# The last chunk of a two-layer block: its attention spread out, its sums, memory part and query products placed later

## What is computed

```python
h = rmsnorm(x, norm_mix_g[l])
p_conv, p_attn, p_ssm = jnp.split(h @ w_in[l], ...)
y_conv = conformer_conv(p_conv, ...)        # sigmoid gate, 31 taps, layer norm, silu
y_attn = stick_breaking_attention(q, k, v)  # 8 heads of 64
y_ssm = s5_ssm(p_ssm, ...)                  # scan, gelu, sigmoid gate
x = x + concat(rmsnorm(y_conv), rmsnorm(y_attn), rmsnorm(y_ssm)) @ w_out[l]
x = x + memory_cross_attention(rmsnorm(x), rmsnorm(mem), w_mq[l], w_mkv[l], w_mo[l])
# peer_ffn, for each chunk of 128 tokens
q = (xc @ w_q)                              # 8 heads; then two scores against 128 keys, top 16 of each
expert = i1 * 128 + i2                      # 16 experts for each token and head
act = gelu(einsum(u_tab[expert], xc))
x = x + einsum(softmax(best) * act, v_tab[expert])
```

## Time and profile before

| | |
|---|---|
| runs | 1736.24 us median, 1735.03 to 1736.36 |
| span of the profiled execution | 1734.4 us |
| PE busy | 1585.6 us, 91% |
| DVE busy | 1211.0 us, 70% |
| ACT busy | 597.7 us, 34% |
| POOL busy | 594.1 us, 34% |
| moved | 680.39 MB, mean 392 GB/s |
| in the chain that ended last | PE 48%, DMA 32%, DVE 13%, ACT 4% |

### The profile page before, as it was taken

One profiled execution on the slowest core, in us unless ns is written; L12 is line 12 of the kernel. 1 busy time (PEld: TensorE's weight loads), 2 busy tenths in 40 slices (PEclk: granted clock), 3 DMA queues, 4 the chain that ended last, 5 costly groups with the idle time before them and its releaser, 6 DMA issues.

```text
span 1734.4 us, 19631 instructions
## 1 busy us (share of the span) xinstructions
PE 1585.6 (91%) x6620; PEld 964.0 (56%) x6620; DVE 1211.0 (70%) x3356; ACT 597.7 (34%) x1445; POOL 594.1 (34%) x527
## 2 busy tenths in 40 slices
PE   8999999999999999998999989999999987777776
PEld 8778866545557777544646547644655643322232
DVE  7721589985886667997557567998657577667665
ACT  4132341553344132254323232255323223222222
POOL 0000153444333332344334343344333444443331
PEclk9999999999999999999999999999999999999999
DMA  9546699999999999999999999999999999999996
GB/s 395 207 146 266 261 386 422 411 407 421 421 422 416 421 421 421 420 416 420 421 422 420 421 422 418 419 370 394 421 421 421 421 421 421 422 421 421 419 420 258
DMA packets 94580, 680.39 MB, mean 392 GB/s; under 512 B 10488, under 2 KB 10768, under 8 KB 12304
## 3 DMA queue, kind: packets, MB, share of 16 engines
q0 software_dynamic: 73728, 536.90, 75.1%
q1 hardware_dynamic: 20752, 142.23, 20.1%
HBM read 678.05 MB, written 1.05 MB: 392 GB/s over the span
## 4 chain that ended last, share of the span: by engine, by line
PE 48%; DMA 32%; DVE 13%; ACT 4%; issue 2%; POOL 0%; DVEq 0%
DMA slots<-expert_rows,expert 32%; PE bank L794 20%; PE bank L403 11%; DVE slots L1680 5%; PE bank L573 4%; PE bank L782 3%; PE bank L779 3%; ACT diag L1226 1%; PE bank L440 1%; DVE sg L1263 1%; PE bank L661 1%; PE bank L411 1%; PE bank L473 1%; DVE cands L1661 1%; DVE htok L1545 1%
## 5 line engine op out<-in xcount | busy, mean ns | idle before, releaser
L794 PE MATMUL bank<-slots,diag 128*128 128x512 f32 x1916 | 906.3, 609 | 130.2 <-ACT diag L1226 124.8
L905 POOL DMA_INDIRECT slots<-expert_rows,expert x512 | 592.2, 1157 | 1115.3 <-PE bank L794 850.7
L1680 DVE CUSTOM_DVE_ANT_0 slots<-slots,htok 128x1024 f32<-128x1024 f32 x512 | 626.3, 1223 | 334.7 <-DMA slots<-expert_rows,expert 324.6
L794 PEld LDWEIGHTS bank<-slots,diag 128*128 128x128 f32 x1916 | 346.9, 192 | 544.4 <-issue 322.3
L1239 ACT ACTIVATE gel<-dot 128x2 f32<-128x2 f32 (+1 forms) x258 | 52.5, 204 | 675.7 <-DVE dot L1680 674.5
L1226 ACT ACTIVATE diag<-ident,coef 128x128 f32<-128x128 f32 x479 | 168.2, 394 | 186.4 <-DVE coef L1263 182.4
L403 PEld LDWEIGHTS bank<-hT,ring 128*128 128x128 f32 x1632 | 198.6, 193 | 44.4 <-issue 44.1
L403 PE MATMUL bank<-hT,ring 128*128 128x128 f32 x1632 | 199.1, 276 | 0.0
L1263 DVE SCALAR_TENSOR_TENSOR coef<-gel,ginv,gexp 128x2 f32<-128x2 f32 (+1 forms) x258 | 54.9, 213 | 60.7 <-ACT gel L1239 59.3
L1239 ACT ACT_TABLE_LOAD x66 | 84.7, 1283 | 1.2
L1263 DVE SCALAR_TENSOR_TENSOR sg<-pad,prm,sg 128x128 f32<-128x128 f32 x240 | 71.7, 344 | 0.0
(11 more groups left out here) (298 smaller groups left out, 1517.7 us busy)
## 6 DMA issues: line engine op xcount, KB each, us to landing
ring<-w_blocks SPq DMA_DIRECT2D x96, 1024.0 KB
slots<-w_blocks SPq DMA_DIRECT2D x26, 1024.0 KB, 8.0
slots<-expert_rows,expert POOLq DMA_INDIRECT x512
kept<-w_blocks SPq DMA_DIRECT2D x4, 1024.0 KB, 12.3
keys<-w_blocks SPq DMA_DIRECT2D x2, 1024.0 KB
prm<-small SPq DMA_DIRECT2D x2, 768.0 KB
x<-x_rows SPq DMA_DIRECT2D x2, 512.0 KB, 11.0
slots<-mem_rows SPq DMA_DIRECT2D x1, 1024.0 KB
```

Of the source, the lines that this page charges most:

```text
L794: last = mm(bank[h][:, :], diag[:, i % DIAGS, :], slots[:, n % SLOTS, D + h * 512:D + (h + 1) * 512], start=m == 0, stop=n == end)
L905: nc.gpsimd.indirect_dma_start(slots[:, n % SLOTS, :], None, experts_d, bass.IndirectOffsetOnAxis(ap=idx[q % 2][:, k:k + 1], axis=0),).the ...
L1680: v.tensor_tensor_reduce(out=slots[:, s, 0:D], in0=slots[:, s, 0:D], in1=htok[:, ph % 2, :], scale=1.0, scalar=0.0, op0=ALU.mult, op1=ALU.add,
```

## The change

Only chunk 3 changes, apart from one buffer. A group of its attention takes 6 ticks and not 4, so that the four groups start at offsets 31, 37, 43 and 49. `LATER` of chunk 3 becomes 14, so that its output product (now offsets 55 to 65), the memory part and the norm before the peer part stand 9 ticks later; `MIXED_LATER` moves the sums and the additions to x by the same 9. The first query product stands at offset 103, the second at 110, the other six 16 ticks apart (126 to 206), within the last stage. The scores follow their product by 4 ticks in the same turn of the loop. The route of query 24 starts at offset 109 and takes two steps a tick, to offset 116. The gains of the last norm are loaded ahead of the sixth query block and no longer behind all blocks, and the squares of the last norm are written to a part of `htok`, as `hT` is still in use.

```diff
-LATER = [0] + [5] * (NST - 1)
+LATER = [0, 5, 5, 14]
+MIXED_LATER = [0, 0, 0, LATER[-1] - LATER[-2]]
 def att_tick(ci, g, step):
-    return BEGIN[ci] + 31 + 4 * g + step if ci else ...
+    return BEGIN[ci] + 31 + (6 if ci == NST - 1 else 4) * g + step if ci else ...
-         [94 + 4 * h for h in range(PH)], [94 + 4 * h for h in range(PH)]]
+         [94 + 4 * h for h in range(PH)], [103] + [110 + 16 * h for h in range(PH - 1)]]
 # group_sums (PE), groups (ACT), mixed (DVE)
-                at = BEGIN[ci]
+                at = BEGIN[ci] + MIXED_LATER[ci]
 # queries (PE) and feed (ACT)
-                    if h and ci:
+                    if ci == NST - 1 and h < PH:
+                        yield at + WQ_AT[ci][h] + 4
+                        scores_of(h)
+                    elif 0 < ci < NST - 1 and h:
                         yield at + WQ_AT[ci][h - 1] + 4
                         scores_of(h - 1)
 # sync
+                if n == FIRST["wq"] + 5 and stage == NST - 1:
+                    full(("gain", 1, NST - 1))
+                    nc.sync.dma_start(gains[:, :], rows_d[L, :, :]).then_inc(rows_in, 16)
...
-            full(("gain", 1, NST - 1))
-            nc.sync.dma_start(gains[:, :], rows_d[L, :, :]).then_inc(rows_in, 16)
 # final (ACT)
-                    act(squares[:, h], x[:, c, h], ACT.Square, ...)
+                    act(htok[:, 0, h], x[:, c, h], ACT.Square, ...)
 # route_tick
+    if q == PH * (NST - 1):
+        return G0 + TOP * (q - 1) + 1 + (n - 1) // 2
     return G0 + TOP * (q - 1) - 6 + (n - 1)
```

More of the change, by code:

```diff
@@ L76 @@
 NEVER = 10 ** 9
-LATER = [0] + [5] * (NST - 1)
+LATER = [0, 5, 5, 14]
+MIXED_LATER = [0, 0, 0, LATER[-1] - LATER[-2]]
 def att_tick(ci, g, step):
-    return BEGIN[ci] + 31 + 4 * g + step if ci else (30, 31, 32, 32, 33, 34, 35, 36)[step] + 3 * g
+    return BEGIN[ci] + 31 + (6 if ci == NST - 1 else 4) * g + step if ci else (30, 31, 32, 32, 33, 34, 35, 36)[step] + 3 * g
 KEYS_AT = [[13 + i * 27 // 18 for i in range(18)] + [40 + i for i in range(8)] + [53 + i for i in range(6)],
@@ L1147, in feed @@
                         done(act(pqT[:, h % 2, :, :], pair_of(name), ACT.Copy), name)
-                    if h and ci:
+                    if ci == NST - 1 and h < PH:
+                        yield at + WQ_AT[ci][h] + 5
+                        scores_of(h)
+                    elif 0 < ci < NST - 1 and h:
                         yield at + WQ_AT[ci][h - 1] + 5
@@ L1210, in final @@
                     eng.wait_ge(x_added, 2 * (NST - NC + c) + i + 1)
-                    act(squares[:, h], x[:, c, h], ACT.Square, accum_out=fss[:, i:i + 1]).then_inc(half_squared, 1)
+                    act(htok[:, 0, h], x[:, c, h], ACT.Square, accum_out=fss[:, i:i + 1]).then_inc(half_squared, 1)
                 eng.wait_ge(half_squared, 2 * c + 2)
```

## The result

The changed kernel takes 1740.84 us (median of 9 runs, 1738.0 to 1742.37); beside it the kernel before takes 1736.78 us (9 runs, 1734.62 to 1738.05). The ratio is 1.002, with a 95% interval of 1.0012 to 1.0028: slower by some 4 us. The forecast was 1734.7 us, in a range of 1730.8 to 1738.7.

What follows compares the result with a forecast made beforehand. The prediction took the 421 GB/s transfer rate as the bound: 1.7 us saved in chunk 3's attention, less 0.2 for queries at the change of stages, makes 1.5, so 1734.7 us, range 1730.8 to 1738.7.

Steps and rivals of the forecast that it cites:

- part 1: Chunk 3's attention at six ticks a group: forecast lengths of two-tick pairs, such as offsets 36 and 37 falling to 3.7 us.
- then less than nothing: Offsets 52 to 57: 12.0 us of DVE work, under 14.9 for six fetches, so no loss and the queue refills.
- the crowded pair: Offsets 50 and 51: ACT gets the fourth group's sigmoids beside the convolution's silu; pair grows from 6.6 to 8.1 us.
- My sum: Chunk 3's attention: pair lengths less 4.98 us, eased by queued fetches, giving 6.0 us lost after against 7.7 before.
- the gain of 1.7 us: Stretch with expert fetches only, in chunk 3's attention: loss falls from 7.7 to 6.0 us.
- rival C: Loss only moves: offsets 50 and 51 cost 8.5 or more, output product or norm a further microsecond; 1736.2 us, chance 0.16.
- The bound: Whole kernel: the full transfer rate of 421 GB/s; the change gains or loses only where that rate is missed.
- the sum of before (7.7): Kernel before, offsets 32 to 51: loss worked out from pair lengths, against 7.9 us from the measured rates.
- 1.8 us of cushion: Start of the attention stretch: lateness that already queued fetches absorb, chosen so the sum comes near 7.9 us.
- Rival B: Queries in the last stage: queue bears only 1.2 us of PE's lateness, 5.6 us lost; 1740.1 us, chance 0.09.
- rival D: Last stage's first scores or indices come late, beyond 7.5 us of cover; 1739.2 us if 12 us late, chance 0.03.
- Rival A: Attention spacing works as a whole, queue smooths the bursts, 3.3 to 4.1 us lost; 1731.8 us, chance 0.25.

Runs made afterwards that it cites:

- e1: Changed kernel with PE's transposes of each chunk 3 attention group ahead of the next group's scores: 1737.09 us, ratio 1.0002.
- e4: Kernel before with only PE's transposes of chunk 3 two ticks later (step 6, not 4): 1743.13 us, ratio 1.0038.
- e5: e1 with the four experts that DVE adds in chunk 2's stage moved eight ticks later: 1736.24 us, ratio 0.9995.
- e10: Changed kernel with five ticks a group in chunk 3's attention, not six: 1745.72 us, ratio 1.0055.
- e13: e10 with PE's order mended as in e1: 1741.44 us, ratio 1.0035.
- e3: Kernel before with the late, spread queries alone (last six products 16 ticks apart): 1736.19 us, ratio 0.9999.
- e6: e1 with the first block of the output product kept at offsets 46 and 48 as before: 1736.96 us, ratio 1.0003.
- e8: e1 with the edits of e5, e6 and e7 together: 1736.71 us, ratio 0.9999.
- e9: e8 with chunk 3's query products close together (offsets 103, then 107 to 125 every 3 ticks): 1735.78 us, ratio 0.9996.
- e12: e8 with DVE adding every fourth expert from 310 to 354, not only to 322: 1736.46 us, ratio 1.0001.
- e7: e1 with the convolution's silu, squares and copies on ACT at offset 52, not 50: 1736.65 us, ratio 1.0001.
- e2: Changed kernel with chunk 3's attention at four ticks a group as before: 1737.26 us, ratio 1.0003.

## Why the prediction was wrong, and where it was right

**The step that failed** is in part 1: "The pair of 36 and 37 falls from 6.4 to 3.7 [...] those of 42 to 49 stay". I moved every step of a group by its ticks, on each engine, and never asked in which order one engine issues steps of two groups. The order of the loop in PE's generator, scores of the next group ahead of this group's transposes, was harmless while both fell in one tick. I costed at nothing what is 1.7 + 2.5 = 4.2 us in two pairs, 3.1 to 3.75 us of the time (e1), and 6.4 us when put alone into the kernel before (1743.13 - 1736.68, e4). The list of rivals didn't have it; "a wait that takes the place of the one removed" should have been looked for at every step that another engine waits for.

**The second step that failed** is "then less than nothing" for offsets 52 to 57, the refilling of the queue. Their length was right: 12.0 us forecast, 12.1 measured in e1 (4.1, 3.3 and 4.7). But in offsets 52 to 59 the rate is 336 and 311 GB/s, and they lose 3.7 us. What lets a fetch start is a free slot, and these come late there. POOL's timeline in e1:

```profile
1187.50 0.93 POOL L918 DMA_INDIRECT slots<-expert_rows,expert  x1 [0.70 <-PE bank L806]
1193.79 1.75 POOL L918 DMA_INDIRECT slots<-expert_rows,expert  x1 [5.36 <-DVE x L1279]
...
1199.77 1.94 POOL L918 DMA_INDIRECT slots<-expert_rows,expert  x1 [2.60 <-PE bank L806]
1204.42 0.94 POOL L918 DMA_INDIRECT slots<-expert_rows,expert  x1 [2.71 <-PE bank L806]
```

With the one at 1195.85 that is four fetches in the 16.9 us up to 1204.42, where 6.8 would fit at 2.49 us each. The slots wait for the crowded pair (the 5.36 us end with DVE's addition of an expert) and then for PE. The kernel before issues hardly more, five in 17.2 us from 1186.7 on, at 416 to 418 GB/s: there weight blocks fill the queues. The expectation of e5_takers put the loss down to PE ending an expert 13 to 16 us behind its dot product. That delay, 13.1 to 17.6 us for experts 318 to 321, is real, but it frees slots only from 1216 us on, behind the dip. For the experts of offsets 52 to 57 it is 8.4 to 10.9 us, and 7.5 to 10.8 before. My sum counted only DVE's time, and neither the slots held nor the missing weight blocks. The forecast loss was 6.0 us, that of e1 is 8.1 (4.5 where 6.0 was forecast, and 3.7 where nothing was), and with it the gain of 1.7 us is gone. This is rival C in its outcome (1736.2; e1 has 1737.09 and a ratio of 1.0002), though not by its price: it decided on a pair of 8.5 us, and the pair took 8.1.

**Right.** The bound: 421 GB/s wherever nothing interferes, and the time follows what is lost when more is lost. Against the kernel before, after loses 5.2 us more and is 4.1 slower, e4 8.1 and 6.4, e10 9.0 and 9.4, e13 4.7 and 5.2. The pair lengths once PE's order is mended, ten of ten within 0.1 us, with the 8.1 us of ACT's crowded pair among them. That the sum of before (7.7) came near the measured 7.9 says little: its 1.8 us of cushion were chosen for that, its last term of 0.3 isn't worked out, and in the ten pairs of e1 the same method is 1.5 us off. Rival B is refuted by e3 and by 421 GB/s in the last stage, and rival D by POOL's waits. Rival B's price had a slip: six query places lie in the last stage, not seven, so 0.8 us each make 4.8 and a time of 1739.3. Rival A had the queue smooth the dip; e1's offsets 52 to 59 show the opposite.

**The switch of tables.** In the rows of e13_att5_order the activation behind each load begins 0.01 us after its end (1176.12 + 1.28, then 1177.41), four times in a row, as in the earlier trace rows; and the pair of 50 and 51 took 8.1 us, as worked out with the load alone. The Trainium skill ("ScalarE: Activation LUTs", "What ACT_TABLE_LOAD costs") counts a drain of 1.38 us besides; neither these rows nor that pair has it. What it asks for under "Table sets: the hidden batching unit", batching by set, fits e13, where a group among other sets goes with a pair of 8.8 us; no run here has the tables alone.

**What stays open.** A smaller dip doesn't turn into time. e5, e6, e8, e9 and e12 lose 6.0, 5.6, 5.6, 4.3 and 3.8 us in the common window against 8.1 before, and all of them lie between 0.9995 and 1.0003 with intervals of about 0.001 to either side. Part of it comes back as a loss at 1400 to 1460 us (2.1, 2.4, 1.1 and 1.4 us in e5, e6, e8 and e9), but not in e12. In e12's profile the last dot product starts 603.3 us behind that of expert 288, against 605.7 before and 604.8 in e1; the median of its 11 runs shows none of this. A single profile can't decide over 2 us: the dot product of expert 288, up to which all programs are the same, starts anywhere from 1116.85 us (e12) to 1121.40 (e8).

One thing the traces do show: the end of the kernel doesn't follow the mean rate. From the dot product of expert 430 to the last one it takes 203.9 to 204.3 us in all fourteen kernels, at mean rates from 403 to 409 GB/s. Before and after:

```profile
1520.58:1724.57 203.99, 153.48 (x345) 60.98 (x346) 134.37 (x346) 48.78 (x140) 73.75 (x75) 1.00 0.97 403
1524.91:1729.02 204.11, 164.19 (x453) 73.92 (x454) 134.21 (x345) 50.37 (x146) 74.97 (x75) 1.00 0.98 408
```

The kernel before has less left to move at that point, by 204 x (408 - 403) / 421 = 2.4 us of transfer, and isn't through with it sooner, though DVE's dot products there wait for fetches in every kernel. So "lost transfer time" as counted here is not lost time one for one, and the bound by the mean rate is too simple for differences of 1 or 2 us. What sets the pace of those fetches, and why the loss at 1400 to 1460 appears in some kernels, stays open. No version tried is measurably faster than the kernel before; the best medians are those of e9 (0.9996) and e5 (0.9995).

## What to carry to other kernels

When an order written out in ticks is stretched, list for each engine the steps in the order in which it issues them, before and after, and check every step that another engine waits for: a producer that slips one tick behind its consumer stalls an in-order engine, and with it all that is queued behind (here the gelu, and with it the path of every expert). In the same tick it can still be late (e10). Check too what each stretched step now meets on the engine with switchable tables. And where a stretch short of transfers is to be made up for later, ask when the steps that free the buffers run there, on whichever engine, and what else fills the queues meanwhile: the work of the engine that was full before doesn't decide it alone. Last, a smaller loss of transfer time in one window is a gain only when the median shows it.

## What the runs showed of the hardware

PE's granted clock fell to its lower level of 1.2 GHz behind a wait of PE, in the midst of an otherwise busy kernel. Windows of the kernel after (the clock is the third number from the end), and PE's timeline in e1_order:

```profile
1178.10:1181.50 3.40, 3.40 (x5) 1.34 (x5) 2.27 (x7) 3.34 (x6) 0.66 (x1) 0.51 1.00 381
...
1191.67 2.96 PE L806 MATMUL bank<-slots,diag 128*128 128x512 f32 x4 [2.73 <-ACT diag L1242]
1195.72 3.78 PE L806 MATMUL bank<-slots,diag 128*128 128x512 f32 x4 [1.10 <-ACT diag L1242]
```

In e1 PE does 0.66 us of work from 1187.2 to 1191.67, with the wait of 2.73 us for ACT's diagonals in the crowded tick at its end. The clock falls during the expert that follows, and the next one takes 3.78 us and not the 1.88 of the earlier trace rows, just where PE should catch up; in the first half of offsets 52 to 59 the clock is 0.58 (after) and 0.59 (e1). In the kernel before it is 1.00 there. In e7, with a wait of 3.47 us in that place, it was 0.83 from 1190 to 1200 us. In e2 it was 0.89 from 1192.1 to 1208.0, its offsets 52 to 59, and the transfers ran at 420 GB/s all the same. So a short fall of the clock doesn't by itself bring a loss; what it costs in e1 was not separated from the rest.
